# A two-layer network in one kernel: a later start of GpSimd in the last head, diagonal blocks copied by ScalarE, spreads inside a projection, and unsplit first products

## What is computed

```python
def _even_layer(x, w_in, ..., w_out):
    nq, kc, vc, ks, vs, kw, vw, ng, nz, hq, hf, hi, hz = split(x @ w_in)
    a = _nsa(nq, kc, vc, ks, vs, kw, vw, ng, ...)
    f = lbh + (1.0 - lbh) * sigmoid(hf)
    k = (1.0 - lbh) * sigmoid(-hf)
    o = _hgrn2(silu(hq), k, log(f), hi)          # decayed products inside a chunk + a state
    o = o * rsqrt(mean(square(o), -1) + LN_EPS) * hg_norm
    return concatenate([a * silu(nz), o * silu(hz)]) @ w_out

def _conv_layer(x, w_in, conv_w, conv_b, ln_g, ln_b, w_out):
    a, b, z = split(x @ w_in, 3)
    c = depthwise_conv(a * sigmoid(b), conv_w) + conv_b
    return (silu(_layernorm(c, ln_g, ln_b)) * silu(z)) @ w_out

for i in range(2):
    y = _even_layer(x, ...) if i == 0 else _conv_layer(x, ...)
    x = _layernorm(DEEPNORM_ALPHA * x + y, post_ln_g[i], post_ln_b[i])
    x = x + (p[i] @ ple_w[i]) * sigmoid(x @ ple_gate_w[i])
```

## Time and profile before

| | |
|---|---|
| Median of 3 runs | 2135.93 us (2132.69 to 2137.01) |
| The profiled execution | 2137.22 us |
| Its span (first to last instruction) | 2135.6 us |
| TensorE busy | 2118.0 us |
| VectorE busy | 1242.8 us |
| ScalarE busy | 798.7 us |
| GpSimd busy | 366.6 us |
| Mean granted TensorE clock | 0.997 of full |

### The profile page before, as it was taken

How to read it: one execution, slowest core, us unless ns; L and a number is a source line. 1 busy time by engine, 2 the same in 40 slices (tenths; PEclk the granted TensorE clock), 3 DMA queues, 4 the chain that set the end, 5 groups by cost and what they waited for, 6 DMA issues and landing times.

```text
span 2135.6 us, 28587 instructions
## 1 busy us (share of the span) xinstructions
PE 2118.0 (99%) x10482; PEld 1737.7 (81%) x10482; DVE 1242.8 (58%) x2096; ACT 798.7 (37%) x979; POOL 366.6 (17%) x193
## 2 busy tenths in 40 slices
PE   9999999999999999999999999999999999999999
PEld 8888888878888887788788888888888788887888
DVE  5224575655755747346643478888888783466432
ACT  4224364463554646122722322222323351227221
POOL 0000000000000003000400024454757430004000
PEclk9999999999999999999999999999999999999999
DMA  8222222122222123322233332222222233222332
GB/s 323 79 99 79 80 79 79 64 74 79 79 79 79 59 79 118 118 85 95 77 126 120 123 114 99 99 99 87 92 98 99 97 141 126 90 98 79 126 120 69
DMA packets 33028, 213.63 MB, mean 100 GB/s; under 512 B 3904, under 2 KB 4176, under 8 KB 9408
## 3 DMA queue, kind: packets, MB, share of 16 engines
q1 hardware_dynamic: 28224, 189.54, 25.2%
q0 software_dynamic: 4448, 22.72, 2.7%
q10 hardware_dynamic: 288, 0.52, 0.1%
HBM read 204.39 MB, written 8.39 MB: 100 GB/s over the span
## 4 chain that ended last, share of the span: by engine, by line
PE 95%; DVE 2%; ACT 1%; issue 1%; DMA 0%; POOL 0%; DVEq 0%; ACTq 0%
PE G L460 88%; PE X L460 5%; PE T L460 1%; PE T L620 1%; DVE a_lo L1223 0%; POOL a_lo L378 0%; ACT w_hi L839 0%; DMA Z<-xT_in 0%; DVE Y L1791 0%; DMA Y<-xT_in 0%; DVE Z L1412 0%; ACT Y L1091 0%; ACT a_hi L843 0%; DVE tmp L1451 0%; DVE Z L1411 0%
## 5 line engine op out<-in xcount | busy, mean ns | idle before, releaser
L460 PE MATMUL G<-a_hi,w_hi 128*128 128x512 f32 (+1 forms) x2800 | 1092.8, 391 | 6.4 <-POOL a_lo L378 3.4
L460 PE MATMUL G<-a_lo,w_hi 128*128 128x512 f32 (+1 forms) x2800 | 1083.0, 387 | 0.0
L460 PE MATMUL G<-a_hi,w_lo 128*128 128x512 f32 x2768 | 1075.7, 389 | 0.0
L839 ACT ACTIVATE w_hi<-w_raw 128x2048 fp32r<-128x2048 f32 x174 | 333.2, 1915 | 1019.6 <-PE G L460 1013.8
L1218 DVE TENSOR_TENSOR w_lo<-w_raw,w_hi 128x2048 fp32r<-128x2048 f32 x127 | 291.2, 2293 | 662.8 <-ACT w_hi L839 657.3
L460 PEld LDWEIGHTS G<-a_hi,w_hi 128*128 128x128 f32 x2800 | 526.9, 188 | 118.2 <-POOL a_lo L378 5.1
L460 PEld LDWEIGHTS G<-a_lo,w_hi 128*128 128x128 f32 x2800 | 527.1, 188 | 107.3 <-issue 1.5
L460 PEld LDWEIGHTS G<-a_hi,w_lo 128*128 128x128 f32 x2768 | 520.5, 188 | 108.4
L1766 DVE SCALAR_TENSOR_TENSOR T<-tmp,par,T 128x512 f32<-128x512 f32 x464 | 306.9, 750 | 0.0
L404 POOL TENSOR_TENSOR w_lo<-w_raw,w_hi 128x2048 fp32r<-128x2048 f32 x46 | 212.4, 4617 | 243.2 <-ACT w_hi L839 243.2
L390 POOL TENSOR_TENSOR a_lo<-Y,a_hi 128x512 fp32r<-128x512 f32 x15 | 19.8, 1352 | 782.5 <-ACT a_hi L843 782.5
(11 more groups left out here) (237 smaller groups left out, 1495.7 us busy)
## 6 DMA issues: line engine op xcount, KB each, us to landing
w_raw<-wall_in SPq DMA_DIRECT2D x174, 1024.0 KB, 4.8
Y<-w_in POOLq DMA_DIRECT2D x2, 2048.0 KB, 17.2
Y<-xT_in POOLq DMA_DIRECT2D x4, 1024.0 KB, 6.7
x_residual<-Y POOLq DMA_DIRECT2D x16, 256.0 KB, 3.7
Y<-x_residual POOLq DMA_DIRECT2D x4, 1024.0 KB, 6.1
out<-Y POOLq DMA_DIRECT2D x15, 256.0 KB, 3.6
w_raw<-wall_in SPq DMA_DIRECT2D x12, 256.0 KB, 8.0
Z<-xT_in SPq DMA_DIRECT2D x6, 512.0 KB, 9.5
```

The costliest lines, as they stand in the source:

```text
L460: return pe.matmul(o, l, r, start=start, stop=stop)
L839: f(w_hi[:, w.slot, :], w_raw[:, w.slot, :], ACT.Copy).then_inc(S("w_hi"), 1)
```

## The change

Five edits:

1. Opening. Twelve warm-up products instead of 17. The first two chunks of both first tiles are multiplied as plain float32 from `w_raw` and `Z`, without a split, and the pair goes on from chunk 2 with other lags. The transfer that reuses `w_raw` waits for these products.
2. GpSimd starts its low parts for the output projection after the last gating operation of the last head.
3. ScalarE, not VectorE, copies the four diagonal blocks to `AT`, in every head, in `prev_hz`; the 16-wide level goes through `near_sum`.
4. The two layers' closing norms: ScalarE rounds chunks up to 7 right after they are made; the splits of the gate tiles stand elsewhere; two evacuations go to the other engine. VectorE waits for two quarters of the residual instead of four before its first tiles, and for the other two later.
5. The convolution's norm: both spreads run inside the following projection's tile, after its chunks 3 and 7.

```diff
-WARM_UP = 17
+WARM_UP = 12
-SIDE_ON_ACT = {0: ((0, 5),), 1: ((0, 6), (0, 7)), 2: ((1, 0),), 3: ((1, 1), (1, 3)), 5: ((1, 5),), 6: ((1, 6),), 8: ((1, 7),)}
-SIDE_ON_DVE = {5: 2, 7: 4}
+SIDE_ON_ACT = {0: ((0, 5),), 1: ((0, 6), (0, 7)), 2: ((1, 1),), 5: ((1, 4), (1, 5)), 6: ((1, 6),), 8: ((1, 7),)}
+SIDE_ON_DVE = {3: 0, 5: 2, 6: 3}
-START_LAG = (2, 2, 2, 2, 2, 2, 3, 3, 3, 4, 4, 5, 5, 5, 6, 6)
+RAW = 2
+START_LAG = (RAW,) * RAW + (1, 1, 1, 1, 2, 2, 3, 3, 4, 4, 5, 5, 6, 6)
...
+            sp.wait_ge(S("raw_used"), 1)
             for q in range(4):
                 sp.wait_ge(*((S("quarter_split"), 2 * q + 1) if q < 3 else (S("w_split"), 1)))
...
+            pool.wait_ge(S("level_ready"), HEADS * LEVELS)
             for c in range(KC - 1):
                 pool.wait_ge(S("act_hi0"), c + 1)
...
+            for k in range(RAW):
+                pe.wait_ge(S(f"x_landed{k}"), 16)
+                if k == 0:
+                    pe.wait_ge(S(quarter_landed(0, 0)), 16)
+                mm(G[0][:, :], w_raw[:, 0, k * P:(k + 1) * P], chunk(Z, k), k == 0, False)
+            pe.wait_ge(S(quarter_landed(1, 0)), 16)
+            for k in range(RAW):
+                last = mm(G[1][:, :], w_raw[:, 1, k * P:(k + 1) * P], chunk(Z, k), k == 0, False)
+            last.then_inc(S("raw_used"), 1)
             gemm_pair(0, 0, "x_split", quarters=True)
...
-                pe.wait_ge(S("level_copied"), h * 4)
+                pe.wait_ge(S("blocks_taken"), h)
                 pe.wait_ge(S("state_ready"), h)
...
-            spread_mean(1, c_diag_d)
-            gemm(Idx(W_CONV + 42), Idx(G_CONV + 42))
-            spread_dev(1)
+            gemm(Idx(W_CONV + 42), Idx(G_CONV + 42), between={3: lambda: spread_mean(1, c_diag_d), 7: lambda: spread_dev(1)})
...
                 f(vi, TB[0][:, :], ACT.Copy).then_inc(S("vi_ready"), 1)
+                act.wait_ge(S("level_copied"), h * 3)
+                for lo in range(0, P, BLOCK):
+                    rows = slice(lo, lo + BLOCK)
+                    last = f(AT.rearrange("p (c n) -> p c n", c=NT)[rows, :, lo:lo + BLOCK], near_sum[rows, :, :], ACT.Copy)
+                last.then_inc(S("blocks_taken"), 1)
...
-                    if j > 4:
+                    if j > 8:
                         x1_high(j - 1)
-                    elif j < 4:
+                    elif j < 8:
                         x1_high(j)
+                    if j in (2, 7):
+                        split(Idx(w + 18 + j // 7))
                     for u, c in SIDE_ON_ACT.get(j, ()):
-                        if (u, c) == (1, 3):
-                            split(Idx(w + 18))
                         ple_out(layer, u, c)
-                    if j == 6:
-                        split(Idx(w + 19))
...
+                        if 2 * half == BLOCK:
+                            dst = near_sum[rows, :, half:BLOCK]
+                        else:
+                            dst = AT.rearrange("p (c n) -> p c n", c=NT)[rows, :, lo + half:lo + 2 * half]
+                        last = dve.tensor_copy(dst, src[rows, :, :])
...
-                    for lo in range(0, P, BLOCK):
-                        rows = slice(lo, lo + BLOCK)
-                        last = dve.tensor_copy(AT.rearrange("p (c n) -> p c n", c=NT)[rows, :, lo:lo + BLOCK], near_sum[rows, :, :])
-                    last.then_inc(S("level_copied"), 1)
...
-                for n in range(4):
+                for n in range(2):
                     dve.wait_ge(S(f"res_landed{n}"), 16 * (layer + 1))
...
+                for n in range(2, 4):
+                    dve.wait_ge(S(f"res_landed{n}"), 16 * (layer + 1))
                 split(Idx(w + 10))
```

More of the change, by code:

```diff
@@ L460, in mm, with gemm @@
                 return pe.matmul(o, l, r, start=start, stop=stop)
-            def gemm(w, g, passing=None):
+            def gemm(w, g, passing=None, between={}):
                 pe.wait_ge(S("w_split"), w.n(1))
@@ L473, in gemm @@
                         last.then_inc(S(passing), 1)
+                    if k in between:
+                        between[k]()
                 last.then_inc(S("gemm_done"), 1)
@@ L503, in gemm_pair @@
             def gemm_pair(w, g, acts, between=None, quarters=False, pair_lag=LAG):
-                seconds = 0
-                for k in range(KC + pair_lag):
+                seconds = RAW if quarters else 0
+                for k in range(seconds, KC + pair_lag):
                     lag = START_LAG[k] if quarters and k < KC else pair_lag
@@ L513, in gemm_pair @@
                         wn, gn = Idx(w + n), Idx(g + n)
-                        if quarters and kn % 4 == 0:
-                            pe.wait_ge(*((S("quarter_split"), kn // 2 + n + 1) if kn < 12 else (S("w_split"), n + 1)))
+                        if quarters and (kn % 4 == 0 or kn == RAW):
+                            pe.wait_ge(*((S("quarter_split"), kn // 4 * 2 + n + 1) if kn < 12 else (S("w_split"), n + 1)))
                         elif kn == 0:
@@ L1438, in take_blocks @@
                         rows = slice(lo, lo + half)
-                        last = dve.tensor_copy(AT.rearrange("p (c n) -> p c n", c=NT)[rows, :, lo + half:lo + 2 * half], src[rows, :, :])
+                        if 2 * half == BLOCK:
[3 more added lines that the diff above has]
+                        last = dve.tensor_copy(dst, src[rows, :, :])
                     last.then_inc(S("level_copied"), 1)
@@ L1552, in head @@
                 take_last()
-                wait_alone(("level_copied", h * 4 + 3))
                 take_blocks(2)
@@ L1696, in second_part @@
                         minus_mean(j + 3)
+                    if j in (1, 7, 9):
+                        split(Idx(w + 17 + (1, 7, 9).index(j)))
                     if j in SIDE_ON_DVE:
                         side_out(layer, SIDE_ON_DVE[j])
-                    if j in (1, 7, 9):
-                        split(Idx(w + 17 + (1, 7, 9).index(j)))
                 def gate(g, j, n_gate):
```

## The result

The changed kernel takes 2121.66 us (median of six runs, 2121.5 to 2129.05), the kernel before 2135.2 us (median of six): ratio 0.9946, 95% interval 0.9935 to 0.9958. The forecast was 2121, range 2116 to 2127.5. The profiled execution took 2121.5 us with a span of 2119.8, so 15.8 us of span are gone.

A forecast was written before the change was run, and what follows sets the result against it. TensorE, busy 2118.0 of 2135.6 us, was taken as the bound. Terms -1.4, -8.7, -2.65 and -2.2 sum to -14.95, from 2137.2 to 2122.3 us; less 1.3 for the median, forecast 2121, range 2116 to 2127.5.

The forecast's parts named there:

- Opening, -1.4: Start of the kernel: raw products let TensorE gain two chunk steps if the supply keeps up, -1.4 us.
- Last head, -8.7: Last head: both TensorE waits, the half clock and the residual chunk's wait go, less 0.5 us allowed, -8.7 us.
- GpSimd's 0.5 us that I allowed: Last head: allowance of 0.5 us against the gain, because GpSimd's low parts start and end later.
- half of the bound: Last head: ScalarE's four diagonal copies were to cost at most 0.62 us each, 2.5 us together.
- Ordinary heads, 0: Seven other heads: ScalarE's split moves about 4 us and VectorE's 2, still early enough for TensorE, zero cost.
- Convolution norm, -2.65: Convolution's norm: TensorE's 0.9 us wait, slow spread and slow next tile go, no new wait, -2.65 us.
- my lower bound: Convolution norm: gain of only 0.9 us if the clock still falls.
- The two other norms, -2.2: Two closing norms: waits on GpSimd's low parts shrink, -0.7 us, and the first norm's half clock goes, -1.5 us.
- From the profile to the median: Whole kernel: profiled execution before lay 1.3 us above the median, so 2122.3 became the forecast 2121 us.
- GpSimd was waited for: Rival, last head: GpSimd becomes what TensorE waits for, giving back 2.5 to 3 us, 2124 us; chance 0.13.
- The half clock did not come elsewhere: Rival: half clock comes somewhere else, varying by run, 1.5 to 3.2 us a stretch, 2123 to 2127; chance 0.15.
- ScalarE's wait in the ordinary heads: Rival, seven ordinary heads: ScalarE's split comes too late, 14 us lost at 2 us beyond cover; chance 0.03.

The follow-up runs named there:

- the kernel with early issues: Changed kernel, but VectorE waits for all four residual quarters at once and GpSimd issues the first three behind low parts 4, 8 and 12: 2129.97 us.

## Why the prediction was right, point by point

- **Opening, -1.4, measured -0.71.** The step that failed is "if the supply keeps up with a TensorE that is 1.37 us ahead". I had checked the supply by its activations, chunk 6 above all, and named that the tightest; it held. The tightest was the bank at 40 us, which hangs on a tile's landing through three VectorE operations; TensorE lost 0.52 us there. The run with the opening undone gives 0.64.
- **Last head, -8.7, measured -9.36.** The mechanism was right, and both edits are needed: either alone leaves a wait of 1.3 to 1.7 us, and none leaves 5.0 plus half clock. Of the 9.36 us, 8.2 lie ahead of chunk 15 (5.04 of waits, 2.9 of half clock where I had 3.2) and 1.16 behind it, at the residual. GpSimd's 0.5 us that I allowed was 0.07, with nothing to spare. I had checked chunks 7 and 14; the tight one was chunk 10, whose low part fell under VectorE's split and took 3.34 us, 2.1 more than alone. That the split stops GpSimd for its whole length was counted rightly. The Trainium skill, "SBUF — State Buffer", section "SBUF: two separate sides", states it as an exclusive lock; the trace agrees, with 3.17 us for the split (the rest of GpSimd's operation, then its own 2.29) and 3.34 for the low part. ScalarE's four copies took 0.32 us each, half of the bound. What I did not see is that the residual's edit, which I booked as 1.0 us of the gain, is what keeps GpSimd's late start from costing 7.3 us.
- **Ordinary heads, 0, measured 0.** From the product at 267 us to that at 772 us both kernels take the same 505.14 us. ScalarE's split of the tile moved from 745.37 to 748.74 us and VectorE's from 749.22 to 750.69; with the 0.71 us of the opening that is 4.1 and 2.2 later in the head, as counted, and still ahead of TensorE.
- **Convolution norm, -2.65, measured -2.67.** The wait, the slow spread and the slow products went; with both spreads put back it returned whole. But of the 2.67, some 1.8 are half clock, and one of three runs of that kernel seems to have met none. An execution of before without it would have gained only the 0.9 here, which was my lower bound.
- **The two other norms, -2.2, measured -2.28 and -0.8.** I counted the waits at half, since "such tight waits rarely all go": 1.71 fell to 0.49 in the first, and where I forecast 0.7 us at chunk 8 there are waits of 0.26 and 0.23. With the old order back, the waits cost 0.7 and 0.8 us, so the order is worth these 1.5 in both norms, and some 1.6 of the first norm's 2.28 are half clock.
- **From the profile to the median.** I took 1.3 us off, since the profiled execution of before lay that far above its median. That of the changed kernel lies 0.2 below its own. The likeliest reason is that the profiled execution had the half clock in three places and the other executions of before not always; they have no trace, so it isn't shown. This error and the 0.85 us by which the terms were too small nearly cancel: the forecast of 2121 was nearer than its parts, and that is luck. The two medians are 13.5 us apart, where the two profiled executions are 15.7.

The rivals: GpSimd was waited for by 0.07 us in the last head, at chunk 10. The half clock did not come elsewhere in the profiled run, but the equal waits with and without it, and the spread of the times of one kernel, point to a matter of the run, as the rival had it. ScalarE's wait in the ordinary heads cost nothing.

Open is why one of six runs of the changed kernel took 2129.05 us. Its excess, 7.5 us, is about what a VectorE split stuck behind GpSimd cost in the last head of the kernel with early issues (4.8 us of wait and some 2.8 of half clock), and so is the 7.2 us by which the slowest run with the norms and the opening put back lies above the profiled one. That is a likeness of size only, as neither run has a trace.

## What to carry to other kernels

Two delays in a row on one engine share one slack: taken out singly, each edit looked worth 1.7 us, together 7.3. Price both together, and each alone, before one is dropped as worth little. Check a helper engine at every chunk that another engine's long operation can fall on, not only at the first and the last. Where a helper engine starts later, follow its queue to the end: here its transfers came together, and a wait downstream went from 1.0 to 7.3 us. A gain ahead of a full DMA queue reaches only as far as the first buffer whose release stands behind a landing; read the in-order engine's list there, not only the operands.

## What the runs showed that I had not expected

- GpSimd and VectorE hold each other up wholly and not fairly. In the changed kernel VectorE's split got in after one GpSimd operation (3.17 us for a split of 2.29); with GpSimd's operations shifted by a transfer's 0.57 us it stood behind four of them in a row, 8.57 us, in a kernel whose ten runs all took 7 us or more longer than the changed one. In the changed kernel the GpSimd operation in whose time the split began was followed by another low part, in the other kernel by the issue of a transfer. Whether that decides it, no run here tells.
- The half clock behind a wait of 1.4 us is no property of the wait: first norm, second norm, neither, in three kernels with the same waits; and the same kernel gives times 1.7 us apart. The Trainium skill, "TensorE: Matmul & The Clock Gate", section "Part 1: The HAM clock gate", says of a kernel's start that where the clock changes differs between runs. These runs show the like in mid-kernel, at 1.5 to 1.9 us a time. So a change that removes such a wait gains the wait in each run and the clock in some.
- A tile's landing in the full queue of the opening came between 32.55 and 35.27 us in kernels whose opening differs little or not at all. The changed opening, with the bank still behind the split, lets TensorE feel it: 0.4 us of wait at a landing of 33.3, 0.6 at 33.7, 2.2 at 35.3, and the last brought a stretch of half clock and cost 3.55 us in all. The old opening had no such wait in the three profiles of it, though none of these had a late landing. Both late landings, 35.19 and 35.27, came on one chip, on which the old opening had its tile at 32.91 us; whether the chip, the run or the changed opening there makes them late is open.
